# A two-layer decoder trunk on one core: the float32r products run over their moving rows from the last column to the first

## The chip, the cores and the metric

The kernel runs on one core of one Trainium2 chip. The metric is the device time of one execution in microseconds. Its engines are TensorE (PE, with its weight loads shown apart as PEld), VectorE (DVE), ScalarE (ACT), GpSimd (POOL) and SyncE (SP), which here issues nearly all DMAs. TensorE's clock can be granted at one of two levels, 1.2 and 2.4 GHz.

## The reference, cut to what matters

The input is 256 tokens of 1024 features in float32; 16 learned meta tokens are put in front, so that 272 tokens (T) run through two layers:

```python
for l in range(DEPTH):                                     # DEPTH = 2, D_FF = 2816
    g = norm_g[l]
    h = h + 0.5 * rmsnorm(swiglu(rmsnorm(h, g[0]), ffn_w_in[l, 0], ffn_w_out[l, 0]), g[1])
    hn = rmsnorm(h, g[2])
    u_pool, q, k, v, gate_pool, gate_attn = jnp.split(hn @ w_in[l], SPLITS, axis=-1)
    y_pool = pool_mixer(u_pool, pool_w_grp[l], pool_scale[l], w_pool_proj[l])
    attn = swa_attention(q, k, v, sinks[l])                # 16 heads, window of 128, meta tokens
    merged = jax.nn.sigmoid(gate_pool) * y_pool + jax.nn.sigmoid(gate_attn) * (attn @ w_attn_proj[l])
    h = h + rmsnorm(merged @ w_o[l], g[3])
    h = h + 0.5 * rmsnorm(swiglu(rmsnorm(h, g[4]), ffn_w_in[l, 1], ffn_w_out[l, 1]), g[5])
return h[:, N_META:]
```

`swiglu(x, w_in, w_out)` is `(silu(gate) * up) @ w_out` with `gate, up` the halves of `x @ w_in`. Everything is float32.

## The kernel before, in words

The activations lie transposed: features on the 128 partitions, tokens along the row. A matrix product therefore has a 128 x 128 block of weights as the stationary operand and a row of tokens as the moving operand, 272 columns in layer 0 and mostly 256 in layer 1, where the meta tokens are no longer wanted in every place (`t0` is then 16). The result stands in a PSUM bank as 128 features x tokens.

To keep float32 accuracy every operand is split into a high and a low part in the type float32r, and a product is three instructions into the same bank: high x high, high weights x low row, low weights x high row (`products`, L551 to L555, and its relatives `high` L584, L615 and `product` L621 to L624). Only the last product of the kernel, the output side of the last feed-forward layer, is turned round: there 128 tokens of the hidden layer are stationary and 512 columns of weights move (`tile`, L805 to L811).

The weights come from HBM in units of up to 1024 x 256 into a ring of four slots (`raw`). For each unit ScalarE rounds it to the high part (`w_hi`, L1009), VectorE subtracts to get the low part (`w_lo`, L1326), and TensorE waits for that (`unit_split`) before the unit's products; when the products of a unit are done the slot is free again (`unit_done`). The order of work on each engine is written out by hand, and semaphores tie the engines together.

Where the moving rows lie is laid out on purpose: `LINE, START = 256, 64`. The rows of `x_hi`, `x_lo`, `hid_hi` and `hid_lo` are 1280 bytes apart (`ROW`) and all begin 64 bytes into a stretch of 256 bytes; a row of 272 tokens ends at byte 1152 counted from such a stretch's start. The rows of `o_hi` and `o_lo` (the attention's output) are 1120 bytes apart, so that each begins at another place in its stretch, and `o_lo` is shifted by 16 bytes more. The rows of `z_hi` and `z_lo` (the pooling branch) are 1104 bytes apart. `bank` rows in PSUM are written from column `t0` to column 272, or all 512 in the last product.

The instructions of attention (`scores`, `turn_p`, `attend`), the transposes, the sums of squares and the spreading of the norms' factors are plain float32 and not among the float32r products.

Of the kernel before, what the change touches and what calls it, by code (L numbers as in the profile page):

```python
# [37 lines left out]
T = META + SEQ  # L38
# [12 lines left out]
KF = FF // P  # L51
# [7 lines left out]
HALF_D = D // 2  # L59
# [38 lines left out]
OPEN_BANKS = (3, 1, 6, 0, 4, 5)  # L98
# [9 lines left out]
def first_columns(n):  # L108

    return blocks(n % NORMS, n // NORMS)[1][0]  # L110
# [64 lines left out]
def trunk(nc, x_columns, norm_columns, norm_g, ffn_w_in, ffn_w_out, w_in, pool_w_grp, w_pool_proj,  # L175
          sinks, w_attn_proj, w_o, geometry, out):
    with ExitStack() as ctx:
        def sb(name, shape, dt=F32):
            return ctx.enter_context(nc.sbuf_tensor(name, shape, dt))
# [10 lines left out]
        x_hi = sb("x_hi", [P, KD, ROW], F32R)[:, :, 0:T]  # L190
        x_lo = sb("x_lo", [P, KD, ROW], F32R)[:, :, 0:T]
# [75 lines left out]
        hid_hi, hid_lo = (ffn_placed[name][0][:, :, 0:T] for name in ("hid_hi", "hid_lo"))  # L267
# [25 lines left out]
        bank = [ctx.enter_context(nc.psum_tensor(f"bank{b}", [P, 512], F32)) for b in range(8)]  # L293
# [248 lines left out]
        def _(pe):  # L542
# [3 lines left out]
            def weights(u, k, mt):  # L546

                s = u % RING
                return [w[:, s, k * UW + mt * P:k * UW + (mt + 1) * P] for w in (w_hi, w_lo)]

            def products(ps, w, a_hi, a_lo, start, stop, t0):  # L551

                pe.matmul(ps[:, t0:T], w[0], a_hi[:, t0:T], start=start, stop=False)  # L553
                pe.matmul(ps[:, t0:T], w[0], a_lo[:, t0:T], start=False, stop=False)  # L554
                return pe.matmul(ps[:, t0:T], w[1], a_hi[:, t0:T], start=False, stop=stop)  # L555

            def unit_split(u, l, more=0):
                pe.wait_ge(lo_done, l * UNITS + u + RING + 1 + more)
# [19 lines left out]
            def deep_three(u, l, q, x_at, starts, banks):  # L578

                for n in range(3):  # L580
                    unit_split(u + n, l)
                cut = first_columns(l * NORMS + q - 1)

                def high(c, k, first, end):  # L584
                    w = weights(u + c // 2, k, c % 2)
                    cols = slice(max(starts[c // 2], first), end)
                    pe.matmul(bank[banks[c]][:, cols], w[0], x_hi[:, k, cols], start=k == 0 and c >= CUT_TILES, stop=False)  # L587
                    pe.matmul(bank[banks[c]][:, cols], w[1], x_hi[:, k, cols], start=False, stop=False)  # L588

                for k in range(KD):  # L590
                    if k == 0:
                        pe.wait_ge(xhi_first, l * 3 + q // 2)
                        for c in range(CUT_TILES):
                            high(c, 0, 0, cut)
                        x_high_tile(x_at, l)
                        for c in range(CUT_TILES):
                            high(c, 0, cut, T)
                        for c in range(CUT_TILES, 6):
                            high(c, 0, 0, T)
                    elif k < HIGH_FIRST:  # L600
                        x_high_tile(x_at + k, l)
                        for c in range(1 if k in EARLY_K[(q - 2) // 2 % 3] else 0, 6):
                            high(c, k, 0, T)
                    x_tile(x_at + k, l)
                    for c in range(6):
                        if (k, c) == SUM_AT:
                            sum_part(q, l, 0)
                        if (k, c) == SPREAD_AT:
                            spread_rms(q, l)
                        if c == 0 and k in EARLY_K[(q - 2) // 2 % 3]:  # L610
                            continue
                        w = weights(u + c // 2, k, c % 2)
                        t0 = starts[c // 2]
                        if k < HIGH_FIRST:
                            pe.matmul(bank[banks[c]][:, t0:T], w[0], x_lo[:, k, t0:T], start=False, stop=False)  # L615
                            continue
                        last = products(bank[banks[c]], w, x_hi[:, k, :], x_lo[:, k, :], False, k == KD - 1, t0)
                        if k == KD - 1:
                            last.then_inc(first_done if c % 2 == 0 else unit_done, 1)

            def first_three():  # L621

                def product(c, k, low_weights, operand, start=False, stop=False):
                    return pe.matmul(bank[OPEN_BANKS[c]][:, 0:T], weights(c // 2, k, c % 2)[low_weights], operand[:, k, :],  # L624
                                     start=start, stop=stop)

                pe.wait_ge(xhi_ready, 1)
                pe.wait_ge(first_hi, 1)
                for c in range(2):
                    product(c, 0, 0, x_hi, start=True)  # L630
                x_tile(0, 0)
                for c in range(2):
                    product(c, 0, 0, x_lo)
                pe.wait_ge(first_lo, 1)
                for c in range(2):
                    product(c, 0, 1, x_hi)
                for k in range(KD):
                    piece = [k in range(s.start, s.stop) for s in OPEN_K].index(True)
                    if k > 0:
                        x_tile(k, 0)  # L640
                    for at, u in enumerate(open_order(piece)):
                        if k + at == 0:
                            continue
                        if k == OPEN_K[piece].start:
                            if piece == LAST_PIECE:
                                unit_split(u, 0)
                            else:
                                pe.wait_ge(first_lo, OPEN_UNITS * piece + at + 1)
                        if (k, u) == OPEN_SUM_AT:
                            pe.wait_ge(consts, 1)  # L650
                            sum_part(0, 0, 0)
                        if (k, u) == OPEN_SPREAD_AT:
                            spread_rms(0, 0)
                        for c in (2 * u, 2 * u + 1):
                            last = products(bank[OPEN_BANKS[c]], weights(u, k, c % 2), x_hi[:, k, :], x_lo[:, k, :],
                                            k == 0, k == KD - 1, 0)
                            if k == KD - 1:
                                last.then_inc(first_done if c % 2 == 0 else unit_done, 1)
# [131 lines left out]
            def end_out(l):  # L790

                u0 = U_FFN_OUT[1]
                for n in range(2):
                    banks = END_BANKS[n]
                    for g, (k0, nk) in enumerate(zip(END_K0, END_K)):
                        u = u0 + 6 * n + g
                        s = u % RING
                        unit_split(u, l)
                        pe.wait_ge(hid_ready, l * 2 * KF + KF + k0 + nk)
                        if g == 0:  # L800
                            unit_before = N_IN - 4 + 2 * n
                            pe.wait_ge(tile_read, l * TILES + T_FFN_IN[1] + 2 * unit_before + 2 + TR0)
                        last_unit = g == len(END_K) - 1

                        def tile(k, b):  # L805
                            cols = slice(META + b * P, META + (b + 1) * P)
                            w = [t[:, s, (k - k0) * HALF_D:(k - k0 + 1) * HALF_D] for t in (w_hi, w_lo)]
                            ps = bank[banks[b]]
                            pe.matmul(ps[:, :], hid_hi[:, k, cols], w[0], start=k == 0, stop=False)  # L809
                            pe.matmul(ps[:, :], hid_hi[:, k, cols], w[1], start=False, stop=False)  # L810
                            return pe.matmul(ps[:, :], hid_lo[:, k, cols], w[0], start=False, stop=k == KF - 1)  # L811

                        if last_unit:
                            for b in range(2):
                                for k in range(k0, k0 + nk):
                                    last = tile(k, b)
                                last.then_inc((y_tok_done, unit_done)[b], 1)
                        else:
                            for k in range(k0, k0 + nk):
                                for b in range(2):  # L820
                                    last = tile(k, b)
                            last.then_inc(unit_done, 1)
                        if n == 0 and g < 4:
                            turn_h(g)
# [1189 lines left out]
CUT_TILES = 1  # L2014
# [58 lines left out]
```

## Time and profile before

| | |
|---|---|
| median of 3 runs | 1175.15 us (1174.69 to 1175.27) |
| profiled execution, its own time | 1174.66 us |
| its span, first to last instruction | 1172.8 us |
| TensorE busy | 1163.3 us, 99% |
| VectorE, ScalarE, GpSimd busy | 733.0, 554.8, 430.8 us |
| DMA | 197.58 MB, mean 168 GB/s; the weights' queue fills 52.4% of the engines' span |
| TensorE's share of the chain that ended last | 92% |

How to read it: "busy" is the time in which an engine has an instruction under way. On TensorE neighbouring matmuls overlap, so the duration of one is longer than the distance to the next; what a stream of them costs is the distance from start to start. The chain that ended last is followed back from the last instruction, at each step to what released it.

### The profile page before, as it was taken

To read this page: it belongs to the slowest core of one execution; us is meant where nothing else is said; L and a number is where in the kernel's file an instruction comes from. 1 tells how busy PE (TensorE), PEld (TensorE's weight loads), DVE (VectorE), ACT (ScalarE), POOL (GpSimd) and SP (SyncE) were. 2 spreads that over 40 slices of the span, in tenths; PEclk is the share of its full clock that TensorE was granted. 3 is DMA by queue.
4 is the path that set the end of the run, shared out by engine and by line. 5 is a ranking of instruction groups with operands and counts; after the bars stand their busy time and mean duration, and the time that the engine had idled before them with its cause. 6 is when DMAs were issued, how large, how long until landed. Compare 5 with 4: busy or idle time off the path is not lost.

```text
span 1172.8 us, 23880 instructions
## 1 busy us (share of the span) xinstructions
PE 1163.3 (99%) x9269; PEld 1136.1 (97%) x9269; DVE 733.0 (62%) x1145; ACT 554.8 (47%) x818; POOL 430.8 (37%) x486
## 2 busy tenths in 40 slices
PE   9999999999999999999999999999999999999997
PEld 8999999999999999999999999999999999999986
DVE  7655546968666965544586555459676769755542
ACT  7433335637554653333454333356375556533441
POOL 1945500007211286551109555000082122955500
PEclk9999999999999999999999999999999999999999
DMA  9754458372365365535646543573723744654550
GB/s 295 257 179 156 147 179 233 123 232 72 91 190 170 108 216 179 170 121 196 205 134 216 179 157 133 189 226 109 247 82 93 213 145 144 216 179 161 189 170 36
DMA packets 197934, 197.58 MB, mean 168 GB/s; under 512 B 4448, under 2 KB 191200, under 8 KB 197856
## 3 DMA queue, kind: packets, MB, share of 16 engines
q1 hardware_dynamic: 197712, 196.44, 52.4%
q8 instruction: 55, 0.90, 0.3%
q14 instruction: 23, 0.19, 0.1%
q10 hardware_dynamic: 144, 0.05, 0.0%
HBM read 195.43 MB, written 1.05 MB: 168 GB/s over the span
## 4 chain that ended last, share of the span: by engine, by line
PE 92%; issue 3%; DVE 2%; ACT 1%; POOL 0%; DMA 0%; SPq 0%; DVEq 0%; ACTq 0%; POOLq 0%
PE bank L553 27%; PE bank L554 27%; PE bank L555 27%; PE bank L811 2%; PE bank L809 2%; PE bank L810 2%; DVE w_lo L1326 1%; PE bank L898 1%; PE bank L893 1%; PE bank L852 1%; PE bank L588 1%; PE bank L587 1%; PE bank L863 1%; PE bank L615 0%; PE bank L855 0%
## 5 line engine op out<-in xcount | busy, mean ns | idle before, releaser
L553 PE MATMUL bank<-x_hi,w_hi 128*128 128x272 f32 (+1 forms) x1991 | 573.8, 288 | 0.8 <-DVE w_lo L1732 0.8
L554 PE MATMUL bank<-x_lo,w_hi 128*128 128x272 f32 (+1 forms) x1991 | 568.4, 285 | 0.0
L555 PE MATMUL bank<-x_hi,w_lo 128*128 128x272 f32 (+1 forms) x1991 | 568.3, 285 | 0.0
L1009 ACT ACTIVATE w_hi<-raw 128x2048 fp32r<-128x2048 f32 (+3 forms) x201 | 339.0, 1693 | 401.7 <-PE bank L555 388.9
L1326 DVE TENSOR_TENSOR w_lo<-raw,w_hi 128x2048 fp32r<-128x2048 f32 (+3 forms) x203 | 420.3, 2076 | 143.2 <-ACT w_hi L1009 142.9
L553 PEld LDWEIGHTS bank<-x_hi,w_hi 128*128 128x128 f32 x1991 | 377.1, 189 | 1.9 <-issue 0.7
L554 PEld LDWEIGHTS bank<-x_lo,w_hi 128*128 128x128 f32 x1991 | 377.2, 189 | 0.3
L555 PEld LDWEIGHTS bank<-x_hi,w_lo 128*128 128x128 f32 x1991 | 377.1, 189 | 0.0
L1943 POOL TENSOR_TENSOR hid_hi<-silu,up_r 128x272 f32 x88 | 142.5, 1619 | 149.8 <-DVE up_r L1520 144.3
L555 PE MATMUL bank<-hid_hi,w_lo 128*128 128x272 f32 x528 | 151.3, 287 | 0.0
L553 PE MATMUL bank<-hid_hi,w_hi 128*128 128x272 f32 x528 | 151.3, 286 | 0.0
L554 PE MATMUL bank<-hid_lo,w_hi 128*128 128x272 f32 x528 | 151.3, 286 | 0.0
L1520 DVE TENSOR_TENSOR up_r<-bank,r 128x272 f32<-128x272 f32 x88 | 38.4, 440 | 105.8 <-PE bank L555 88.4
L554 PEld LDWEIGHTS bank<-hid_lo,w_hi 128*128 128x128 f32 x528 | 99.5, 188 | 0.0
L555 PEld LDWEIGHTS bank<-hid_hi,w_lo 128*128 128x128 f32 x528 | 99.5, 188 | 0.0
L553 PEld LDWEIGHTS bank<-hid_hi,w_hi 128*128 128x128 f32 x528 | 99.5, 188 | 0.0
L1512 DVE TENSOR_TENSOR gate_r<-bank,r 128x272 f32<-128x272 f32 x85 | 36.5, 438 | 88.6 <-PE bank L555 88.5
L1948 POOL TENSOR_TENSOR hid_lo<-hid_f,hid_hi 128x272 f32 x88 | 84.5, 961 | 20.0 <-POOL hid_f L1945 20.0
L1945 POOL TENSOR_TENSOR hid_f<-silu,up_r 128x272 f32<-128x272 f32 x88 | 88.8, 1009 | 0.0
L1933 POOL TENSOR_TENSOR rt<-var,half 128x3 f32<-128x3 f32 x6 | 6.1, 1016 | 159.4 <-DVE var L1372 159.4
L1929 POOL TENSOR_TENSOR acc<-acc,sq 128x272 f32<-128x272 f32 x20 | 22.8, 1139 | 95.5 <-ACT sq L1019 94.4
L1979 POOL TENSOR_TENSOR acc<-s,stats 128x16 f32<-128x16 f32 x64 | 19.1, 298 | 89.3 <-DVE stats L1673 89.0
(219 smaller groups left out, 1323.5 us busy)
## 6 DMA issues: line engine op xcount, KB each, us to landing
raw<-in_ffn_w_in SPq DMA_DIRECT2D x84, 1024.0 KB, 5.0
raw<-in_w_in SPq DMA_DIRECT2D x24, 1024.0 KB, 5.6
raw<-in_ffn_w_out SPq DMA_DIRECT2D x24, 768.0 KB, 4.2
raw<-in_ffn_w_out SPq DMA_DIRECT2D x24, 640.0 KB, 3.9
raw<-in_ffn_w_out SPq DMA_DIRECT2D x10, 1024.0 KB, 5.0
raw<-in_w_in SPq DMA_DIRECT2D x16, 512.0 KB, 5.2
raw<-in_w_attn_proj SPq DMA_DIRECT2D x32, 256.0 KB, 4.3
raw<-in_w_o SPq DMA_DIRECT2D x8, 1024.0 KB, 5.6
```

The lines of the kernel that those rows point to most:

```text
L553: pe.matmul(ps[:, t0:T], w[0], a_hi[:, t0:T], start=start, stop=False)
L554: pe.matmul(ps[:, t0:T], w[0], a_lo[:, t0:T], start=False, stop=False)
L555: return pe.matmul(ps[:, t0:T], w[1], a_hi[:, t0:T], start=False, stop=stop)
L809: pe.matmul(ps[:, :], hid_hi[:, k, cols], w[0], start=k == 0, stop=False)
L810: pe.matmul(ps[:, :], hid_hi[:, k, cols], w[1], start=False, stop=False)
L1009: last = act.activation(hi, w, ACT.Copy)
L1326: last = dve.tensor_tensor(lo, w, hi.bitcast(F32), ALU.subtract)
L1512: dve.tensor_tensor(gate_r[:, j, :], bank[4 * (unit // 2 % 2) + j if banks is None else banks[j]][:, 0:T], r[:, :], ALU.mult).then_inc(til ...
L1520: dve.tensor_tensor(up_r[:, j, :], bank[banks[j]][:, 0:T], r[:, :], ALU.mult).then_inc(tile_read, 1)
L1943: pool.tensor_tensor(hid_hi[:, ds(i * 2 + j, 1), :].rearrange("p o t -> p (o t)"), silu[:, j, :], up_r[:, j, :], ALU.mult).then_inc(hid_hi ...
L1945: pool.tensor_tensor(hid_f[:, j, :], silu[:, j, :], up_r[:, j, :], ALU.mult).then_inc(hf_ready, 1)
L1948: pool.tensor_tensor(hid_lo[:, ds(i * 2 + j, 1), :].rearrange("p o t -> p (o t)"), hid_f[:, j, :], hid_hi[:, ds(i * 2 + j, 1), :].rearrang ...
```

## The change

A helper `backwards` takes the place of the direct call in all float32r products. It hands `matmul` a view of the PSUM row and a view of the moving row that both run from the last column to the first. Column i of the row still meets column i of the bank. The stationary operand is given as before, and so are the flags that start and end an accumulation. In `high` the slice of columns becomes a pair of numbers. The plain float32 matmuls and transposes keep their direction. The instructions of every engine stand in the same order as before, with the same shapes, banks and buffers; only the line numbers differ, and `products`, `high`, L615, `product` and `tile` now all issue from the helper's one line.

```diff
--- before.py
+++ after.py
@@ -548,11 +548,16 @@
                 s = u % RING
                 return [w[:, s, k * UW + mt * P:k * UW + (mt + 1) * P] for w in (w_hi, w_lo)]
 
+            def backwards(ps, w, a, first, end, start, stop):
+
+
+                return pe.matmul(ps[:, first:end][:, ::-1], w, a[:, first:end][:, ::-1], start=start, stop=stop)
+
             def products(ps, w, a_hi, a_lo, start, stop, t0):
 
-                pe.matmul(ps[:, t0:T], w[0], a_hi[:, t0:T], start=start, stop=False)
-                pe.matmul(ps[:, t0:T], w[0], a_lo[:, t0:T], start=False, stop=False)
-                return pe.matmul(ps[:, t0:T], w[1], a_hi[:, t0:T], start=False, stop=stop)
+                backwards(ps, w[0], a_hi, t0, T, start, False)
+                backwards(ps, w[0], a_lo, t0, T, False, False)
+                return backwards(ps, w[1], a_hi, t0, T, False, stop)
 
             def unit_split(u, l, more=0):
                 pe.wait_ge(lo_done, l * UNITS + u + RING + 1 + more)
@@ -583,9 +588,9 @@
 
                 def high(c, k, first, end):
                     w = weights(u + c // 2, k, c % 2)
-                    cols = slice(max(starts[c // 2], first), end)
-                    pe.matmul(bank[banks[c]][:, cols], w[0], x_hi[:, k, cols], start=k == 0 and c >= CUT_TILES, stop=False)
-                    pe.matmul(bank[banks[c]][:, cols], w[1], x_hi[:, k, cols], start=False, stop=False)
+                    first = max(starts[c // 2], first)
+                    backwards(bank[banks[c]], w[0], x_hi[:, k, :], first, end, k == 0 and c >= CUT_TILES, False)
+                    backwards(bank[banks[c]], w[1], x_hi[:, k, :], first, end, False, False)
 
                 for k in range(KD):
                     if k == 0:
@@ -612,7 +617,7 @@
                         w = weights(u + c // 2, k, c % 2)
                         t0 = starts[c // 2]
                         if k < HIGH_FIRST:
-                            pe.matmul(bank[banks[c]][:, t0:T], w[0], x_lo[:, k, t0:T], start=False, stop=False)
+                            backwards(bank[banks[c]], w[0], x_lo[:, k, :], t0, T, False, False)
                             continue
                         last = products(bank[banks[c]], w, x_hi[:, k, :], x_lo[:, k, :], False, k == KD - 1, t0)
                         if k == KD - 1:
@@ -621,8 +626,8 @@
             def first_three():
 
                 def product(c, k, low_weights, operand, start=False, stop=False):
-                    return pe.matmul(bank[OPEN_BANKS[c]][:, 0:T], weights(c // 2, k, c % 2)[low_weights], operand[:, k, :],
-                                     start=start, stop=stop)
+                    return backwards(bank[OPEN_BANKS[c]], weights(c // 2, k, c % 2)[low_weights], operand[:, k, :], 0, T,
+                                     start, stop)
 
                 pe.wait_ge(xhi_ready, 1)
                 pe.wait_ge(first_hi, 1)
@@ -806,9 +811,9 @@
                             cols = slice(META + b * P, META + (b + 1) * P)
                             w = [t[:, s, (k - k0) * HALF_D:(k - k0 + 1) * HALF_D] for t in (w_hi, w_lo)]
                             ps = bank[banks[b]]
-                            pe.matmul(ps[:, :], hid_hi[:, k, cols], w[0], start=k == 0, stop=False)
-                            pe.matmul(ps[:, :], hid_hi[:, k, cols], w[1], start=False, stop=False)
-                            return pe.matmul(ps[:, :], hid_lo[:, k, cols], w[0], start=False, stop=k == KF - 1)
+                            backwards(ps, hid_hi[:, k, cols], w[0], 0, HALF_D, k == 0, False)
+                            backwards(ps, hid_hi[:, k, cols], w[1], 0, HALF_D, False, False)
+                            return backwards(ps, hid_lo[:, k, cols], w[0], 0, HALF_D, False, k == KF - 1)
 
                         if last_unit:
                             for b in range(2):
```

## Rows read from the trace of the kernel before

**Rows 1.** The page, part 1: busy time, share of the span, instructions, by engine.

```profile
PE 1163.3 (99%) x9269; PEld 1136.1 (97%) x9269; DVE 733.0 (62%) x1145; ACT 554.8 (47%) x818; POOL 430.8 (37%) x486
```

**Rows 2.** The page, part 2: granted clock of TensorE in 40 slices, in tenths.

```profile
PEclk9999999999999999999999999999999999999999
```

**Rows 3.** The waits on TensorE: in total us, times, longest us.

```profile
PE bank L986 <- DVE r L1318: 1.2, 1, 1.2
...
PE bank L553 <- DVE w_lo L1732: 0.8, 2, 0.5
```

**Rows 4.** The waits of all engines: ScalarE's split of the weights.

```profile
ACT w_hi L1009 <- PE bank L555: 388.9, 124, 4.6
```

**Rows 5.** Groups of instructions by shape, TensorE: busy us, mean ns | idle before.

```profile
L553 PE MATMUL bank<-x_hi,w_hi 128*128 128x272 f32 x1401 | 404.9, 289 | 0.8 <-DVE w_lo L1732 0.8
...
L553 PE MATMUL bank<-x_hi,w_hi 128*128 128x256 f32 x590 | 168.9, 286 | 0.0
...
L553 PE MATMUL bank<-hid_hi,w_hi 128*128 128x272 f32 x528 | 151.3, 286 | 0.0
...
L809 PE MATMUL bank<-w_hi,hid_hi 128*128 128x512 f32 x88 | 34.7, 394 | 0.0
...
L553 PE MATMUL bank<-o_hi,w_hi 128*128 128x272 f32 x70 | 20.3, 290 | 0.0
...
L553 PE MATMUL bank<-o_hi,w_hi 128*128 128x256 f32 x70 | 19.9, 284 | 0.0
...
L587 PE MATMUL bank<-x_hi,w_hi 128*128 128x272 f32 x39 | 10.1, 291 | 0.0
...
L553 PE MATMUL bank<-z_hi,w_hi 128*128 128x272 f32 x32 | 9.6, 299 | 0.0
...
L553 PE MATMUL bank<-z_hi,w_hi 128*128 128x256 f32 x32 | 9.3, 290 | 0.0
...
L615 PE MATMUL bank<-x_lo,w_hi 128*128 128x272 f32 x43 | 6.6, 287 | 0.0
...
L587 PE MATMUL bank<-x_hi,w_hi 128*128 128x256 f32 x14 | 3.6, 285 | 0.0
...
L615 PE MATMUL bank<-x_lo,w_hi 128*128 128x256 f32 x15 | 2.4, 283 | 0.0
```

**Rows 6.** Order in time, TensorE, 60 us: start us, duration us, line.

```profile
59.77 0.29 PE L554 MATMUL bank<-x_lo,w_hi 128*128 128x272 f32 x1
...
60.88 0.28 PE L554 MATMUL bank<-x_lo,w_hi 128*128 128x272 f32 x1
```

**Rows 7.** Order in time, TensorE, 1050 us.

```profile
1049.83 0.28 PE L555 MATMUL bank<-x_hi,w_lo 128*128 128x256 f32 x1
...
1050.91 0.28 PE L555 MATMUL bank<-x_hi,w_lo 128*128 128x256 f32 x1
```

**Rows 8.** Order in time, TensorE, 1140 us.

```profile
1139.72 0.39 PE L811 MATMUL bank<-w_hi,hid_lo 128*128 128x512 f32 x1
...
1140.85 0.39 PE L810 MATMUL bank<-w_lo,hid_hi 128*128 128x512 f32 x1
```

**Rows 9.** Order in time, TensorE, the products of o in layer 0.

```profile
346.48 0.29 PE L554 MATMUL bank<-o_lo,w_hi 128*128 128x272 f32 x1
...
349.74 0.29 PE L553 MATMUL bank<-o_hi,w_hi 128*128 128x272 f32 x1
```

**Rows 10.** Order in time, TensorE, the products of o in layer 1.

```profile
930.78 0.28 PE L553 MATMUL bank<-o_hi,w_hi 128*128 128x256 f32 x1
...
933.99 0.28 PE L553 MATMUL bank<-o_hi,w_hi 128*128 128x256 f32 x1
```

**Rows 11.** Order in time, TensorE, products of 128 columns near 207 us.

```profile
207.00 0.27 PE L588 MATMUL bank<-x_hi,w_lo 128*128 128x128 f32 x1
207.11 0.28 PE L587 MATMUL bank<-x_hi,w_hi 128*128 128x144 f32 x1
```

## The prediction

> **What bounds the kernel now.** I read four views. First the page's busy times and its row of the granted clock: TensorE is busy 1163.3 of 1172.8 us [rows 1] and is granted its upper level, 2.4 GHz, in all forty slices [rows 2]. Second the waits. TensorE's largest wait for another engine is 1.2 us, before its first instruction, and the only one in front of the float32r products is 0.8 us, twice, both at the opening [rows 3]. In the other direction ScalarE stands still 388.9 us before its splits of the weights until TensorE has given a slot back [rows 4]. So the weights are split ahead, everybody waits for TensorE, and the time is the sum of what the products cost. Third the groups by shape, for the counts [rows 5]. Fourth the order in time, for what one product costs. The busy time of one (289 ns) is no price here, since neighbouring products overlap; the price is the distance from one start to the next:
> - 272 columns, rows of x: nine distances between 59.77 and 60.88, 1.11 / 9 = 0.1233 us [rows 6].
> - 256 columns, rows of x: nine between 1049.83 and 1050.91, 0.1200 us [rows 7].
> - 512 columns (the last product, where the weights are what moves): five between 1139.72 and 1140.85, 0.226 us [rows 8].
>
> Counts from [rows 5], each line of the helper standing for three instructions (L553, L554 and L555 have the same counts): 272 columns, 3 x (1401 + 528 + 70 + 32) + 2 x 39 + 43 = 6214. 256 columns, 3 x (590 + 70 + 32) + 2 x 14 + 15 = 2119. 512 columns, 3 x 88 = 264. The sum is 6214 x 0.1233 + 2119 x 0.1200 + 264 x 0.226 = 766.2 + 254.3 + 59.7 = 1080.2 us, 92% of the span; 26 further float32r products at the opening and in cut tiles are left out as too few. The rest of the span is attention, transposes, the sums of squares, the opening and the end, none of which the change touches. The profiled execution took 1174.66 us by its own time, 1.9 us beside its span, and 0.5 us under the median of the runs, 1175.15; I forecast against the median.
>
> **The change part by part.** It adds no instruction, no wait, no DMA and no byte; every product reads and writes the same columns, in falling order. Three things can move: the reading of the moving row, the writing of PSUM, and how the end of one product meets the start of the next. The loading of the weights is left as it was. No row of before shows an operand of TensorE read or written in falling order, so all three are bounded from both sides.
>
> What a product costs divides into columns and a rest. From 256 to 512 columns it costs 0.226 - 0.120 = 0.106 us more, 0.414 ns a column, or a column at each tick of 2.4 GHz. So 272 columns are 0.1126 us and a rest of 0.0107; 256 columns 0.1060 and a rest of 0.0140; 512 columns 0.2120 and a rest of 0.0140.
>
> - Columns, upper end: the pace per column halves. 6214 x 0.1126 + 2119 x 0.1060 + 264 x 0.2120 = 699.7 + 224.6 + 56.0 = +980.3 us. Lower end: nothing, because a column at every tick is already all that the granted clock has.
> - The rest, lower end: it goes entirely, except that no product comes closer to the next than the 0.11 us at which a product of 128 columns is followed (207.00 to 207.11), which is what a load of weights allows [rows 11]. That is 6214 x 0.0107 + 2119 x 0.0100 + 264 x 0.0140 = 66.5 + 21.2 + 3.7 = -91.4 us, to 1083.8.
> - The rest, as the rows show it vary: it depends on where the rows lie. The rows of x and of the hidden layer all begin 64 bytes into a 256-byte stretch, those of o begin at another place for every k. With the same 272 columns and the same engine the o products stand 26 distances in 349.74 - 346.48 = 3.26 us, 0.1254 each [rows 9], that is 0.0021 more; with 256 columns 27 distances in 933.99 - 930.78 = 3.21 us, 0.1189 each [rows 10], 0.0011 less. So the layout decides one or two nanoseconds, in both directions, and a reversal could do as much.
>
> I take zero for the columns and zero for the rest. For the columns: a reversed row touches the same addresses and each address has the same neighbour before or behind it; only an engine that looks for a rising step in particular could tell. For the rest: at the seam a product now ends at byte 1152 of its row and the next begins at byte 64; reversed it ends at 64 and the next begins at 1152. The jump has the same length, and with k's rows 1280 bytes apart (five stretches of 256) both seams lie in the same way. If what costs the rest is this jump, its mirror costs the same. That is an argument by symmetry, not a row, and the bounds stay.
>
> What hides the edit is nothing: TensorE has no slack, so each nanosecond a product is 5908 x 0.001 = 5.9 us on the products of 272 columns over x and the hidden layer (3 x 1929 + 78 + 43 = 5908). If TensorE became quicker, ScalarE's split would be late next, and it has 388.9 us to give [rows 4]; nothing takes a gain of some per cent away. If it became slower, nothing would give it back.
>
> **A rule against the change.** The rows show a column per tick into PSUM, and all of those products write rising columns [rows 6 to 8]. The Trainium skill (Advanced Engine Details and Errata, section Memory Cachelines, PSUM Cachelines) says that PSUM works in lines of 8 bytes, two float32 values, that every two consecutive elements should be contiguous and that any non-contiguous pattern slows matmuls significantly. Whether a falling row is contiguous in that sense it leaves open. Read as two elements of one line, one after the other, it is (the rows have even ends) and the time stays at 1175; read as a step of plus one, it isn't, and the time is that of the third rival. No run here shows it so far.
>
> **The rivals.**
> 1. *The seam or a meeting of two reads costs more.* [...] For it: the layout moves the rest, and the place of the x rows is the cheaper one of the two seen with 272 columns, so a new arrangement is likelier to lose than to win there. Against it: the addresses are the same. Price: 272 columns over x and the hidden layer at the 0.1254 of the o rows: 5908 x 0.0021 = +12.4, 1187.6.
> 2. *The rest gets smaller.* For it: with 256 columns the x rows are the dearer place, and the rest of 0.0107 to 0.0140 is mostly avoidable in principle. Price, with the same difference downward and the 1813 products of 256 columns over x (3 x 590 + 28 + 15) at 0.1189: -12.4 - 2.0 = -14.4, 1160.8.
> 3. *A falling row runs at half pace*, in the read or in the write. It decides at every single product, so it comes wholly or not at all: 1175.15 + 980.3 = 2155 us. For it: two float32 values together may be what gives a column per tick. Against it: no row shows it, and the same two values still arrive one behind the other.
> 4. *It doesn't do what it says.* If the falling pattern were turned into a rising one before it reached the chip, the time would be 1175.15; this gives the forecast's number and is held within it.
>
> **How the numbers follow.** What a measurement of this kernel can tell from no change is about 0.2%, 2.35 us, or 0.27 ns a product over 8597 products. Forecast, no change: 0.30. Rival 1: 0.24. Rival 2: 0.26. Rival 3: 0.20. The time is that of the likeliest, 1175.2, its own range 1172.8 to 1177.5. The range for all takes in rivals 1 and 2 with about twice their prices, since only two layouts bound them: 1146 to 1205. Rival 3 stays outside, with its 0.20. Faster by over 0.2%: 0.26; within: 0.30; slower: 0.24 + 0.20 = 0.44.
>
> **What would show it.** Right: distances of 0.1233, 0.1200 and 0.226 us in the same three stretches and the same waits. Rival 1 or 2: the three distances changed by one or two nanoseconds, unlike for 272 and 256 columns. Rival 3: distances of 0.236, 0.226 and 0.438, TensorE still at 99% and the idle time of all others about doubled. I am wrong in my argument, whatever the time, if the distance of 272 columns changes by more than 0.3 ns: then direction matters and the symmetry is gone.

## The result, and the profile after

The changed kernel takes 1183.19 us (median of 4 runs, 1182.80 to 1184.83) where the kernel before took 1174.95 beside it: a ratio of 1.0073, 95% interval 1.0055 to 1.0090, or 8.2 us more. That is inside the stated range, but outside the forecast's own range, 1172.8 to 1177.5 us, which is what no change allows. The profiled execution has a span of 1181.0 us against 1172.8. Two executions among the runs below stand apart and are left out of the ratios: one of e_256 with 6544.71 us and one of e_at64 with 1418.74 us, at a granted clock of 0.753.

The page of the changed kernel, parts 1 and 2, which answer to [rows 1, 2]:

```profile
PE 1171.4 (99%) x9269; PEld 1142.4 (97%) x9269; DVE 732.0 (62%) x1145; ACT 554.8 (47%) x818; POOL 427.6 (36%) x486
...
PEclk9999999999999999999999999999999999999999
```

TensorE's busy time grows by 8.1 us and the span by 8.2; VectorE and ScalarE work as long as before, and the granted clock is the same. The waits of the changed kernel (engine, line and releaser: us in total, times, longest us), which answer to [rows 3, 4]:

```profile
PE bank L991 <- DVE r L1323: 1.2, 1, 1.2
...
PE bank L554 <- DVE w_lo L1737: 1.1, 2, 0.7
...
ACT w_hi L1014 <- PE bank L554: 403.5, 125, 4.7
```

No wait took the place of anything: TensorE's waits for other engines are 3.2 us in all, as before, and ScalarE waits 14.6 us longer for it. So the 8.2 us lie in the price of a product, the distance from its start to the next. The order in time of the changed kernel, first and last row of four stretches (start us, duration us, engine, line), which answer to [rows 6, 7, 8, 9]:

```profile
59.72 0.29 PE L554 MATMUL bank<-x_hi,w_lo 128*128 128x272 f32 x1
...
62.22 0.29 PE L554 MATMUL bank<-x_lo,w_hi 128*128 128x272 f32 x1
...
1059.81 0.28 PE L554 MATMUL bank<-x_hi,w_hi 128*128 128x256 f32 x1
...
1066.91 0.28 PE L554 MATMUL bank<-x_hi,w_hi 128*128 128x256 f32 x1
...
1149.70 0.40 PE L554 MATMUL bank<-w_lo,hid_hi 128*128 128x512 f32 x1
...
1153.20 0.40 PE L554 MATMUL bank<-w_lo,hid_hi 128*128 128x512 f32 x1
...
350.07 0.29 PE L554 MATMUL bank<-o_hi,w_hi 128*128 128x272 f32 x1
...
353.32 0.29 PE L554 MATMUL bank<-o_hi,w_lo 128*128 128x272 f32 x1
```

Twenty distances in 2.50 us are 0.1250 each (before 0.1233), sixty in 7.10 us are 0.1183 (before 0.1200), fifteen in 3.50 us are 0.2333 (before 0.226, or 0.2267 over the fifteen up to the row below), and twenty-six of the o rows in 3.25 us are 0.1250 (before 0.1254). The row of before, in order of time, fifteen products behind the first of [rows 8]:

```profile
1143.12 0.39 PE L811 MATMUL bank<-w_hi,hid_lo 128*128 128x512 f32 x1
```

With the counts of the prediction: 5908 x 0.0017 = +10.0, 1813 x -0.0017 = -3.1, 264 x 0.0066 = +1.7, together +8.6 us, where 8.2 are measured. Over the whole traces, with all distances between neighbouring products of one kind taken and gaps left out, the means are 123.4 and 125.0 ns for 272 columns over x and the hidden layer, 120.0 and 118.6 for 256 over x, 227.3 and 233.4 for 512: nearly the same picture, a little smaller in each. The o rows get 0.3 ns cheaper and those of z 0.7 dearer with 272 columns, which is under 0.1 us each. The change is thus two losses and one gain.

### The profile page after: what moved, and what is told of

The parts are those of the page before. It is cut to its first block, busy times and chain, and to the rows that moved or that the text cites. A ratio compares the mean times of both kernels' runs of the same rounds, so it can differ in the third digit from the quotient of the medians.

```text
span 1181.0 us, 23880 instructions
## 1 busy us (share of the span) xinstructions
PE 1171.4 (99%) x9269; PEld 1142.4 (97%) x9269; DVE 732.0 (62%) x1145; ACT 554.8 (47%) x818; POOL 427.6 (36%) x486
## 4 chain that ended last, share of the span: by engine, by line
PE 94%; issue 3%; DVE 2%; ACT 1%; DMA 0%; POOL 0%; SPq 0%; DVEq 0%; ACTq 0%; POOLq 0%
PE bank L554 88%; PE bank L903 1%; PE bank L898 1%; DVE w_lo L1331 1%; PE bank L857 1%; PE bank L705 1%; PE bank L868 0%; PE bank L860 0%; DMA raw<-in_ffn_w_in 0%; PE bank L913 0%; PE bank L901 0%; PE bank L869 0%; PE bank L870 0%; PE bank L731 0%; ACT w_hi L1014 0%
## 5 line engine op out<-in xcount | busy, mean ns | idle before, releaser
L554 PE MATMUL bank<-x_hi,w_hi 128*128 128x272 f32 (+1 forms) x2056 | 592.3, 289 | 1.1 <-DVE w_lo L1737 1.1
L554 PE MATMUL bank<-x_hi,w_lo 128*128 128x272 f32 (+1 forms) x2056 | 586.7, 287 | 0.0
L554 PE MATMUL bank<-x_lo,w_hi 128*128 128x272 f32 (+1 forms) x2051 | 579.7, 287 | 0.0
L554 PEld LDWEIGHTS bank<-x_hi,w_hi 128*128 128x128 f32 x2056 | 387.4, 188 | 2.6 <-DVE x_lo L1420 0.9
L554 PEld LDWEIGHTS bank<-x_hi,w_lo 128*128 128x128 f32 x2056 | 387.2, 188 | 0.0
L554 PEld LDWEIGHTS bank<-x_lo,w_hi 128*128 128x128 f32 x2051 | 383.4, 188 | 0.3
L1953 POOL TENSOR_TENSOR hid_lo<-hid_f,hid_hi 128x272 f32 x88 | 91.4, 1039 | 20.0 <-POOL hid_f L1950 20.0
L1950 POOL TENSOR_TENSOR hid_f<-silu,up_r 128x272 f32<-128x272 f32 x88 | 79.5, 903 | 0.0
```

Source lines behind the costliest of these rows:

```text
L554: return pe.matmul(ps[:, first:end][:, ::-1], w, a[:, first:end][:, ::-1], start=start, stop=stop)
L1950: pool.tensor_tensor(hid_f[:, j, :], silu[:, j, :], up_r[:, j, :], ALU.mult).then_inc(hf_ready, 1)
L1953: pool.tensor_tensor(hid_lo[:, ds(i * 2 + j, 1), :].rearrange("p o t -> p (o t)"), hid_f[:, j, :], hid_hi[:, ds(i * 2 + j, 1), :].rearrang ...
```

## The experiments

Two theories stood against each other. The read theory: a product's price depends on how its moving row is read, that is on the direction and on the place, within a stretch of 256 bytes, where the read begins and ends. The write theory: a falling row in PSUM is dearer. They were to be told apart in the kernel and in streams of products by themselves.

"Place" below means the byte within its stretch of 256 at which a row, or a block of weights, begins. In the trunk the weights' place is 128 (streams with this place give the trunk's prices, below); the rows of x begin at 64 with 272 columns and at 128 with 256, since the 16 meta tokens in front are left out.

**m1_streams.** The row, the bank, or both fall. This is the core of the kernel, cut; its 36 products a setting use one row of each of two tiles and eight blocks of weights in turn:

```diff
+ for s, (n, place, w_place, kind) in enumerate(streams()):
+     ... 36 products: (w_hi, hi), (w_hi, lo), (w_lo, hi), twelve times
+     if kind == "rise":         pe.matmul(ps, w, row)
+     elif kind == "fall":       pe.matmul(turned(ps, True), w, turned(row, True))
+     elif kind == "read falls": pe.matmul(ps, w, turned(row, True))
+     else:                      pe.matmul(turned(ps, True), w, row)
```

> Not the trunk: 36 float32r products in a stream for each setting (a row's place in its 256 bytes, columns, place of the weights), in four kinds: row and bank rising, both falling, only the row falling, only the bank falling. Read theory (the cost lies in how the row is read, and at which place of the 256 bytes a product's read begins and ends): at the kernel's places the streams repeat the trunk, 272 columns at 64 bytes 0.1233 rising and 0.1250 falling, 256 at 128 bytes 0.1200 and 0.1184, 512 at 128 bytes 0.2267 and 0.2333; 'only the row falling' equals 'both falling' and 'only the bank falling' equals rising; the distance changes with the place by some 0.004 us, differently for the two directions. Write theory (the falling bank costs): the other way round, 'only the bank falling' equals 'both falling', and the place matters alike in both directions. Rival on the column count: falling costs more per column (272 and 512 dearer, in proportion), then the excess grows steadily from 128 to 512 columns.

The order in time of this kernel for 272 columns at 64 bytes, weights at 128: rising (L81), both falling (L83), only the row (L85), only the bank (L87), each from its seventh product to its last, 29 distances:

```profile
210.54 0.28 PE L81 MATMUL bank<-x_hi,w_hi 128*128 128x272 f32 x1
...
214.12 0.29 PE L81 MATMUL bank<-x_hi,w_lo 128*128 128x272 f32 x1
...
215.00 0.29 PE L83 MATMUL bank<-x_hi,w_hi 128*128 128x272 f32 x1
...
218.62 0.29 PE L83 MATMUL bank<-x_hi,w_lo 128*128 128x272 f32 x1
...
219.50 0.29 PE L85 MATMUL bank<-x_hi,w_hi 128*128 128x272 f32 x1
...
223.12 0.29 PE L85 MATMUL bank<-x_hi,w_lo 128*128 128x272 f32 x1
...
224.00 0.29 PE L87 MATMUL bank<-x_hi,w_hi 128*128 128x272 f32 x1
...
227.57 0.28 PE L87 MATMUL bank<-x_hi,w_lo 128*128 128x272 f32 x1
```

3.58, 3.62, 3.62 and 3.57 us: the falling row makes the difference, the falling bank none. The settled distances, from the second third of each stream on, in ns from the starts in this trace (weights at 128 bytes):

```
columns, place   rising   both fall   row falls   bank falls
272, 64          123.3    125.0       125.0       123.4
256, 128         120.0    118.4       118.4       120.0
512, 128         226.7    233.3       233.3       226.7
256, 192         113.4    120.0       120.0       117.8
272, 128         125.4    124.5       124.5       125.6
512, 64          233.3    233.4       233.4       233.4
128 to 240, 128  111.4 to 112.1   111.5 to 111.7
320, 128         146.7    146.7
384, 128         173.3    177.9
448, 128         202.7    206.9
```

The first three rows are the trunk's three prices, before and after, each within 0.3 ns. The next three show that the place decides which direction is cheaper: one cannot say that falling costs more. At 192 bytes 256 rising columns cost 113.4 or, in the stream beside it whose reads are the same and whose bank falls, 117.8. Of the other 23 pairs of streams with a rising row, which differ in the bank alone, three disagree by more than half a nanosecond too, by 0.9 to 1.4 ns (256 columns at 0 and 160, 272 at 96), and the falling bank is the cheaper in two of them. No falling bank is needed for that: in m2_places below, rising streams of 256 columns cost 117.8 at 192 bytes and 116.7 at 160, where the rising ones of this run cost 113.4 and 117.8, and those of 272 columns at 96 bytes 126.6 instead of 125.3. The rival by columns fails as well: at 128 bytes the excess of falling over rising is 1.4 at 288 columns, 0.0 at 320, 4.6 at 384, 4.2 at 448 and 6.6 at 512; at 64 bytes falling is 1.8 cheaper at 288 and equal at 512.

**e_read and e_write**, the same question in the trunk:

```diff
- return pe.matmul(ps[:, first:end][:, ::-1], w, a[:, first:end][:, ::-1], start=start, stop=stop)
+ return pe.matmul(ps[:, first:end], w, a[:, first:end][:, ::-1], start=start, stop=stop)   # e_read
+ return pe.matmul(ps[:, first:end][:, ::-1], w, a[:, first:end], start=start, stop=stop)   # e_write
```

> Only the moving row is read last token first, the bank is written in rising order; so the tokens of each result are mirrored, and the output is not the reference's. Read theory: 1183.2 us, the time of the changed kernel, with distances 0.1250, 0.1184 and 0.2333 us. Write theory: 1175.0, the time of before.

> Only the bank is written last token first, the row is read in rising order; the results are mirrored here too. Read theory: 1175.0 us with the distances of before (0.1233, 0.1200, 0.2267). Write theory: 1183.2 us.

e_read took 1182.79 us (2 runs), a ratio of 1.0067 (1.0048 to 1.0085) to 1174.89 beside it; e_write 1175.03, 1.0001 (0.9991 to 1.0011). The order in time of e_read, 272 columns:

```profile
59.80 0.29 PE L554 MATMUL bank<-x_hi,w_hi 128*128 128x272 f32 x1
...
62.30 0.29 PE L554 MATMUL bank<-x_hi,w_lo 128*128 128x272 f32 x1
```

The order in time of e_write, 272 columns:

```profile
59.74 0.28 PE L554 MATMUL bank<-x_hi,w_lo 128*128 128x272 f32 x1
...
62.21 0.28 PE L554 MATMUL bank<-x_lo,w_hi 128*128 128x272 f32 x1
```

Twenty distances in 2.50 us against 2.47. The write theory has fallen.

**e_256, e_272, e_512**, the change for one width alone:

```diff
+ step = -1 if end - first == 256 else 1          # 272 and 512 in the other two
+ return pe.matmul(ps[:, first:end][:, ::step], w, a[:, first:end][:, ::step], start=start, stop=stop)
```

> The change only where a product has 256 columns. In the changed kernel's trace these fell from 0.1200 to about 0.1184 us. If the three kinds of products add up independently: 1813 x -0.0016 = -2.9 us, 1172.1 us, a ratio of 0.9975. Rival (the gain comes from a falling product standing behind a falling one of another width, or is taken back by waits, since VectorE and ScalarE must keep up in layer 1): no difference, 1175.0 us.

> The change only where a product has 272 columns. From the streams (0.1233 rising, 0.1250 falling at the kernel's place): 5908 x 0.00174 = +10.3 us, less what the o and z products give, 1185 us, more than the whole change costs. Rival (interplay between kinds): 1183, the time of the whole change.

> The change only in the last product, 512 columns of weights moving. From the streams (0.2267 rising, 0.2333 falling): 264 x 0.0066 = +1.7 us, 1176.7 us. Rival (no effect, since the last product waits for splits): 1175.0.

Measured: e_256 1172.62 us, 0.9982 (0.9973 to 0.9991), -2.3 us; e_272 1183.57, 1.0078 (1.0061 to 1.0095) to 1174.75, +8.8; e_512 1176.74, 1.0017 (1.0007 to 1.0027), +2.0. The three add up to +8.5, the whole change made +8.2: within their intervals, one or two us each, the kinds are independent. For e_272 the expectation was 1.5 us too high. Half of that its trace explains: over all 272-column products of x the mean distance rises by 1.6 ns, not 1.74, so that 5908 products make +9.5. The products of o and z, which it did not price, cancel (-0.07 and +0.07 us), and 0.7 us stay open. The order in time of e_256, sixty distances in 7.10 us, as in the changed kernel:

```profile
1049.75 0.28 PE L555 MATMUL bank<-x_lo,w_hi 128*128 128x256 f32 x1
...
1056.85 0.28 PE L555 MATMUL bank<-x_lo,w_hi 128*128 128x256 f32 x1
```

**m2_places** asks whether the row's place counts by itself or against that of the weights:

```diff
+ table = [(n, place, w, kind) for n in OWN for w in (128, 0, 64, 192) for place in range(0, 256, 16)
+          for kind in KINDS[:2]]                  # 18 products each
```

> Not the trunk: streams of 18 float32r products, row places in steps of 16 bytes for four places of the weights (128, 0, 64, 192), rising and falling, 256, 272 and 512 columns. Theory (two reads meet in the same 256-byte pattern: the row and the weights): only the difference between the place of the row and that of the weights matters, so the table for weights at 64 is that for weights at 128 shifted by 64 bytes, and 256 rising keeps one cheap place, 0.1134 us, at 64 bytes behind the weights' place. Rival (each read has its own cost by its own place): the cheap place stays at 192 whatever the weights' place is.

The order in time of this kernel, 512 rising columns, eleven distances each: row at 64 and weights at 128, both at 128, both at 64.

```profile
634.75 0.40 PE L79 MATMUL bank<-x_hi,w_hi 128*128 128x512 f32 x1
...
637.32 0.39 PE L79 MATMUL bank<-x_hi,w_lo 128*128 128x512 f32 x1
...
668.48 0.39 PE L79 MATMUL bank<-x_hi,w_hi 128*128 128x512 f32 x1
...
670.98 0.39 PE L79 MATMUL bank<-x_hi,w_lo 128*128 128x512 f32 x1
...
903.53 0.39 PE L79 MATMUL bank<-x_hi,w_hi 128*128 128x512 f32 x1
...
906.03 0.39 PE L79 MATMUL bank<-x_hi,w_lo 128*128 128x512 f32 x1
```

2.57, 2.50 and 2.50 us: the cheap place goes with the weights. So it does in the whole table. Three of its 24 rows, in ns (rising, places 0, 16, ... 240):

```
256, weights at 128: 119.8 118.6 117.3 119.4 113.3 119.1 118.0 116.8 120.0 118.6 116.7 118.2 117.8 119.5 119.5 113.4
256, weights at  64: 113.4 119.0 118.0 116.8 120.0 118.5 116.7 118.2 117.8 119.5 119.5 113.4 118.8 118.9 117.3 119.4
272, weights at 128: 126.8 124.5 123.5 123.5 123.4 126.0 126.6 124.9 126.5 124.3 125.4 126.4 126.6 125.1 124.8 126.6
```

The second row is the first shifted by four places, which are 64 bytes, within 0.3 ns but for one value that is off by 1.0. Of all 384 streams, both directions, 376 are within 0.3 ns of the others with the same difference of places; the eight that aren't (by up to 1.8 ns) stand at places 0 to 32, at the beginning of a block of the table, where something else had run before them than before their counterparts. So the difference of the two places counts, in turns of 256 bytes, falling as well as rising: the price over the bare columns hangs on two streams of reads, the row's and the weights'. Where in the chip they meet no run shows. The expected cheap place, 64 bytes behind the weights', did not come back: in m1_streams 256 columns cost 113.4 there (192 bytes) and 117.8 at 64 bytes, in this run 117.8 and 113.3, and a second cheap place lies 112 behind, at 240. In the falling direction 256 columns never cost under 117.5 and 272 never under 124.4, against 113.3 and 123.3 rising. In this table before's 256 columns stand on the dearest rising place, 128, and its 272 columns on the cheapest, 64.

**e_at192 and e_at64** put this to use in the trunk, with everything rising:

```diff
+ MOVE = 16                                        # words: e_at192; 48 in e_at64, 28 in e_at240
+ class Rows:
+     def __getitem__(self, key):
+         return self.tile[:, :, self.at["now"]:self.at["now"] + T][key]
- x_hi = sb("x_hi", [P, KD, ROW], F32R)[:, :, 0:T]
+ x_hi = Rows(sb("x_hi", [P, KD, ROW], F32R), x_at)        # x_lo likewise
+ x_at["now"] = MOVE * l                           # on each engine, before the mixer's norm
```

> Everything rises as before; from the mixer's norm of layer 1 on, the rows of x_hi and x_lo lie 64 bytes further on, so that the 1813 products of 256 columns begin at 192 instead of 128 bytes of their stretch (the weights' place is 128), and 192 products of 272 columns in that part begin at 128 instead of 64. Place theory with the stream that settled at 0.1134 us: 1813 x -0.0066 + 192 x 0.0021 = -11.6, 1163.2 us. The same with the other stream's 0.1178 for this place: 1813 x -0.0022 + 0.4 = -3.6, 1171.2. Rival (what made 256 columns cheaper in the reversed kernel was the direction, not where a read begins and ends): 1174.9, the time of before.

> The same, but the rows of x lie 192 bytes further on, so that the products of 256 columns begin at 64 bytes and the 192 products of 272 columns at 0. The streams gave 0.1134 in one run and 0.1178 in the other for this place too, and 0.1267 for 272 columns at 0. Place theory: 1163.5 with the cheap one, 1171.6 with the dear one; if the two kernels differ from each other, which of two settled patterns a stream falls into depends on what ran before it. Rival: 1174.9.

e_at192 took 1170.98 us, 0.9964 (0.9952 to 0.9977) to 1175.01, e_at64 1170.49, 0.9955 (0.9940 to 0.9970), both near the dear one of the two prices that their expectations gave. No product falls in them, so the rival is refuted: 256 columns get cheaper by place without any change of direction. The order in time of e_at192:

```profile
1049.83 0.28 PE L569 MATMUL bank<-x_hi,w_lo 128*128 128x256 f32 x1
...
1056.90 0.28 PE L569 MATMUL bank<-x_hi,w_lo 128*128 128x256 f32 x1
```

Sixty distances in 7.07 us, 0.1178. The order in time of e_at64, two stretches of twenty distances:

```profile
984.77 0.28 PE L569 MATMUL bank<-x_hi,w_lo 128*128 128x256 f32 x1
...
987.04 0.28 PE L568 MATMUL bank<-x_lo,w_hi 128*128 128x256 f32 x1
...
1049.77 0.28 PE L569 MATMUL bank<-x_hi,w_lo 128*128 128x256 f32 x1
...
1052.13 0.28 PE L568 MATMUL bank<-x_lo,w_hi 128*128 128x256 f32 x1
```

0.1135 in the one and 0.1180 in the other: the same products at the same places, in one execution, at two prices. Five of its six executions range from 1167.12 to 1172.41 us, all five of e_at192 from 1170.85 to 1172.05; that the two prices make the wider spread is likely, but not shown.

**m3_preludes and e_at240** follow that up. Each stream of 36 rising products of 256 columns stands behind a prelude, 18 products of 272 columns at one of 16 places:

```diff
+ for place in (64, 192, 240, 128):
+     for before in range(0, 256, 16):
+         table += [(272, before, 128, "rise"), (256, place, 128, "rise"), (256, place, 128, "rise")]
```

> Not the trunk: 36 rising products of 256 columns at place 64, 192, 240 or 128 (weights at 128), each stream behind 18 products of 272 columns at one of 16 places. Theory of two settled patterns: at 64, 192 and 240 some streams settle at 0.1134 us and others at 0.1178 us or thereabouts, by what ran before, and none in between; at 128 all are at 0.1200. Rival (drift with time, or a chance that has nothing to do with what ran before): within one stream the distance changes, or all streams of a place agree.

> As e_at192, with the rows of x 112 bytes further on, so that 256 columns begin at 240 bytes and 192 products of 272 columns at 176. The stream at 240 settled at 0.1134 us. If the trunk's streams settle there too: 1813 x -0.0066 + 192 x 0.0031 = -11.4, 1163.5 us; if they settle in the dearer pattern, as they did at 192: about 1171.

The order in time of m3_preludes, each stream from its tenth product on, 26 distances: place 64 behind a prelude at 0, place 64 behind one at 16, place 240 behind one at 64.

```profile
41.39 0.28 PE L81 MATMUL bank<-x_hi,w_hi 128*128 128x256 f32 x1
...
44.33 0.28 PE L81 MATMUL bank<-x_hi,w_lo 128*128 128x256 f32 x1
...
47.76 0.28 PE L81 MATMUL bank<-x_hi,w_hi 128*128 128x256 f32 x1
...
50.82 0.28 PE L81 MATMUL bank<-x_hi,w_lo 128*128 128x256 f32 x1
...
273.11 0.28 PE L81 MATMUL bank<-x_hi,w_hi 128*128 128x256 f32 x1
...
276.06 0.28 PE L81 MATMUL bank<-x_hi,w_lo 128*128 128x256 f32 x1
```

2.94, 3.06 and 2.95 us. Of sixteen streams at 64 nine settle at 113.4 ns and seven at 117.8; at 192 one and fifteen; at 240 all sixteen at 113.4; at 128 all between 119.9 and 120.2. Once settled, a stream keeps its price. Each prelude ran once, so this run alone could not tell its effect from chance; in m2_places, though, the same order of differences came by four times, with four places of the weights, and the stream 64 before the weights settled at 113.3 or 113.4 all four times, the one 64 behind at 117.8. So what ran before picks the price. In the trunk e_at240 took 1165.95 us, a ratio of 0.9919 (0.9905 to 0.9932) to 1175.00, 9.1 us less than before and the best of all versions here. Its order in time, sixty distances in 6.80 us, 0.1133:

```profile
1049.81 0.28 PE L569 MATMUL bank<-x_hi,w_lo 128*128 128x256 f32 x1
...
1056.61 0.28 PE L569 MATMUL bank<-x_hi,w_lo 128*128 128x256 f32 x1
```

The gain is 2.4 us short of the 11.4 expected. Part of that is given back as waits of TensorE (in total us, times, longest us):

```profile
PE bank L567 <- DVE w_lo L1751: 2.2, 2, 1.3
PE bank L1000 <- DVE r L1336: 1.2, 1, 1.2
PE bank L737 <- DVE rt L1406: 1.0, 2, 0.7
PE bank L714 <- DVE acc L1428: 0.8, 1, 0.8
PE bank L740 <- POOL rt L1952: 0.3, 1, 0.3
```

They are 5.5 us together. Before, the two of [rows 3] and two others made 3.2, so 2.3 us are new in this execution, most of them for the split of the weights and the sum of squares: VectorE's work begins to show. The settling costs something as well, since the m3 streams at 240 take up to 14 products until they are cheap: over the whole trace the mean distance of the 256-column products of x is 113.8 ns, not 113.3, which is 0.8 us over 1813 products. The two together are 3.1 us, in an execution that was 0.9 above the median, so they account for the missing 2.4 within what executions differ by.

## Why the prediction was right or wrong

**The time.** The forecast was no change, and the kernel is 8.2 us slower. The stated range held because the rivals were priced into it; the likeliest case had the mechanism wrong.

**The bound.** Right (the waits at the opening are 0.8 us in sum, not each). TensorE alone sets the time; in all nine variants of the trunk the time followed the prices of the products, within 2.4 us. That nothing takes a gain of some per cent away was too strong: in e_at240, 9.1 us quicker, waits mostly for VectorE, not ScalarE, took 2.3 us back.

**The columns.** Right to take zero for a halved pace, and rival 3 is refuted: no product of any run cost near 0.236 us for 272 columns. But the division into 0.414 ns a column and a fixed rest was too simple. Falling at 128 bytes, 320 to 512 columns cost (233.3 - 146.7) / 192 = 0.451 ns a column, rising 0.417. The extra at this place thus grows with the row, though unevenly, and isn't one fixed step at the seam; where along the row it arises no run shows.

**The rest, taken as zero by symmetry.** This is the step that failed. The argument looked at the row alone. Even there the jump has the same length only from a row to itself (1088 bytes, back or forward); to the row of the next k in the same tile it is 192 bytes rising and 2368 falling, and the mirror holds only in turns of 256 bytes. That length isn't what costs: the streams of m1_streams make no such step to a next k and have the trunk's prices. m2_places shows that the price hangs on the row's place less the weights' place; the change turned the row and left the weights, so the pair has no mirror. The test stated for it, more than 0.3 ns on 272 columns, came out at 1.7.

**Rival 1** is what happened, in kind and nearly in size: 5908 x 0.0021 = +12.4 was stated for 272 columns, 0.0017 and +8.8 us (e_272) measured. Its reason, a meeting of two reads, is borne out by m2_places, as far as the price hangs on the places of both. Its hint, that the x rows stood on one of the cheaper places, was the best evidence there was, and deserved more than 0.24. **Rival 2** is what happened to the 256 columns: -2.3 us in e_256 against 1813 x 0.0011 = 2.0 priced. Both at once had not been priced as a case; since the row has a different place in the two layers, it was the natural one.

**The last product** was priced with the others and is dearer by 0.0066 us, the largest step of the three. Its place with equal 128 for row and weights is the cheapest of all for 512 rising columns (226.6 against 228.8 to 236.5), which could only have been lost.

**The rule on PSUM.** A falling bank costs nothing, 1.0001 (0.9991 to 1.0011). The Trainium skill (Advanced Engine Details and Errata, section Memory Cachelines, PSUM Cachelines) asks that every two consecutive elements be contiguous; a falling row of even length and even start meets that, so by the looser reading of the rule the trace agrees; read as a step of plus one, the rule would not hold here.

## What to carry to other kernels

When TensorE is never idle, read the distance between the starts of its products to the nanosecond: a few per cent can lie between it and its columns. Try the place of the moving rows against that of the weights, width by width, in a stream of products by itself, which gave the trunk's three prices in both directions within 0.3 ns. Where a stream has two settled prices it can't say which one the kernel will take: try several preludes. And move rows per stage, since a row cut at its front has another place. An argument by symmetry must hold for everything that is read at the time, not only for what the change turns.

## What was not expected of the hardware

- A float32r product of 256 columns costs 113.3 to 120.3 ns and one of 272 columns 123.3 to 127.1, by the difference of two addresses within 256 bytes, the direction and what ran before, at a granted clock of 0.999 to 1.0 (m1_streams, m2_places).
- The same stream has two settled prices, 113.4 and 117.8 ns, at some places, and what ran before it picks one; at 240 bytes (112 behind the weights) all sixteen streams of m3_preludes found the cheap one.
- From 128 to 240 columns the price is flat at 111.4 to 112.1 ns, so 256 columns at 113.4 are within 2 ns of it. That flat price is taken here for the load of the weights; no run took the loads away.
